# Two-layer hybrid decoder step on one core: gate and up units of the feed-forward as four token blocks of 264, sent in two pairs of seven block products

## The reference, cut to what matters

```python
h = _rmsnorm(x, P['norm_ffn_g'][layer]) * (1 + mod[:, 4]) + mod[:, 3]
gu = h @ P['ffn_w_gate_up'][layer]
x = x + mod[:, 5] * ((jax.nn.silu(gu[..., :FFN_HIDDEN]) * gu[..., FFN_HIDDEN:]) @ P['ffn_w_down'][layer])
```

## Time and profile before

| | |
|---|---|
| runs (3) | 2440.2 us median, 2438.15 to 2442.3 |
| span of the profiled execution, first to last instruction | 2437.2 us |
| PE busy | 2379.8 us, 98% |
| DVE, ACT, POOL busy | 1170.9, 694.2, 773.4 us |
| one turn of the loop in layer 1, from one up unit's end to the next's (1869.42 to 1934.81) | 65.4 us |

### The profile page before, as it was taken

The page is one execution under the profiler, slowest core; times in us unless marked ns, Lnnn a source line. Parts: engine busy times, 40 slices in busy tenths (PEclk is TensorE's granted clock), DMA queues, the critical chain, the costliest instruction groups (busy, mean ns, idle before and its releaser), DMA issues.

```text
span 2437.2 us, 37047 instructions
## 1 busy us (share of the span) xinstructions
PE 2379.8 (98%) x15703; PEld 2268.7 (93%) x15703; DVE 1170.9 (48%) x2223; ACT 694.2 (28%) x1056; POOL 773.4 (32%) x652
## 2 busy tenths in 40 slices
PE   7999999999999999999999999999999999999998
PEld 5998878578999999999999999999999999999998
DVE  5277653557434444434446321546544444444445
ACT  5112324426222222212224211144421222122224
POOL 3231111113334433333333332133343343333431
PEclk9999999989999999999999999999999999999999
DMA  9424443960222222222222688311111111111111
GB/s 313 157 68 145 126 132 103 312 210 23 70 87 87 68 72 70 87 70 87 87 70 70 216 283 302 104 37 35 35 53 52 36 52 52 37 51 52 53 53 72
DMA packets 163970, 249.12 MB, mean 102 GB/s; under 512 B 6165, under 2 KB 150826, under 8 KB 162527
## 3 DMA queue, kind: packets, MB, share of 16 engines
q1 hardware_dynamic: 150762, 179.29, 22.4%
q0 software_dynamic: 4784, 63.31, 7.5%
q10 hardware_dynamic: 8260, 4.15, 0.6%
HBM read 228.04 MB, written 62.54 MB: 119 GB/s over the span
## 4 chain that ended last, share of the span: by engine, by line
PE 78%; DVE 1%; ACT 1%; issue 0%; ACTq 0%; DVEq 0%
PE ps L2844 32%; PE ps L2884 12%; PE ps L2882 12%; PE ps L2883 11%; PE ps L3034 4%; PE ps L2988 3%; PE ps L3169 1%; PE ps L3057 1%; PE ps L3361 0%; PE ps L3204 0%; DVE x L1875 0%; PE ps L3378 0%; PE ps L3078 0%; PE ps L3071 0%; DVE tmp L2435 0%
## 5 line engine op out<-in xcount | busy, mean ns | idle before, releaser
L2844 PE MATMUL ps<-h_hi,w_slot 128*128 128x352 f32 x2112 | 537.6, 328 | 3.0 <-DVE acc_s L1966 1.4
L2635 POOL TENSOR_TENSOR w_slot<-w_raw,w_slot 128x512 fp32r<-128x512 f32 x240 | 304.1, 1300 | 679.5 <-DVE w_sum L2028 552.5
L2844 PE MATMUL ps<-f_hi,w_slot 128*128 128x352 f32 x1920 | 467.7, 323 | 0.0
L2884 PE MATMUL ps<-h_hi,w_slot 128*128 128x352 f32 x1280 | 413.0, 323 | 0.0
L2882 PE MATMUL ps<-h_hi,w_slot 128*128 128x352 f32 x1280 | 412.8, 323 | 0.0
L2883 PE MATMUL ps<-h_lo,w_slot 128*128 128x352 f32 x1280 | 411.2, 321 | 0.0
L1965 DVE SCALAR_TENSOR_TENSOR x<-ps,mod,x 128x704 f32<-128x704 f32 (+1 forms) x384 | 270.6, 747 | 288.0 <-PE ps L2844 287.6
L2844 PEld LDWEIGHTS ps<-h_hi,w_slot 128*128 128x128 f32 x2112 | 370.2, 188 | 22.0 <-issue 18.8
L2844 PE MATMUL ps<-h_lo,w_slot 128*128 128x352 f32 x1056 | 339.2, 321 | 0.0
L2844 PEld LDWEIGHTS ps<-f_hi,w_slot 128*128 128x128 f32 x1920 | 333.8, 188 | 4.9 <-issue 4.1
L2621 POOL TENSOR_TENSOR w_slot<-w_raw,w_slot 128x512 fp32r<-128x512 f32 x132 | 178.4, 1377 | 490.1 <-ACT w_slot L1389 481.7
(11 more groups left out here) (399 smaller groups left out, 3209.3 us busy)
## 6 DMA issues: line engine op xcount, KB each, us to landing
w_raw<-in_ada_w SPq DMA_DIRECT2D x48, 1024.0 KB, 5.6
w_raw<-in_ffn_w_gate_up SPq DMA_DIRECT2D x44, 1024.0 KB, 5.1
out_kv_sample<-in_cache_b_kv POOLq DMA_DIRECT2D x8, 4088.0 KB, 21.5
w_raw<-in_ffn_w_down SPq DMA_DIRECT2D x22, 1024.0 KB, 4.9
w_raw<-in_e_w_in SPq DMA_DIRECT2D x11, 1024.0 KB, 5.6
w_raw<-in_o_w_in SPq DMA_DIRECT2D x10, 1024.0 KB, 17.5
cache<-in_cache_b_kv SPq DMA_DIRECT2D x16, 512.0 KB, 6.4
out_kv_sample<-in_cache_b_kv POOLq DMA_DIRECT2D x8, 1016.0 KB, 9.9
```

The lines of the kernel that those rows point to most:

```text
L2635: pool.tensor_tensor(w_slot[slot_of(it.raw)][:, c], w_raw[it.raw.slot][:, c], w_slot[it.hi[0]].bitcast(F32)[:, c], ALU.subtract).then_inc( ...
L2844: mm = pe.matmul(big(t)[:, b, 0:BLK], wt, xt[:, k, b * BLK:b * BLK + BLK], start=(k == 0 and n == 0), stop=(k == K - 1 and n == 2))
L2884: return pe.matmul(bank(it, j), w_low, x_high, start=False, stop=last, skip_group_check=True)
```

## The change

`BLK` blocks in the gate and up units of groups 1 to 10 become four blocks of `QB` = 264 tokens. They form two pairs: pair 1 (blocks 2 and 3) and pair 0 (blocks 0 and 1). Each pair is done by seven products. A unit is then 14 products of 12 matmuls of 264, in the order P1, P4, P2, P5, P6, P7, P3 of pair 1, then the same of pair 0. A slot of weights is given back after P2 of pair 0, a slot of sums after P3 of pair 0. ACT and DVE handle the results pair by pair. The sums of tokens cover 528 tokens each. The second half of the plain up unit's result leaves later (`hidden_rest`, after `t_rest` and the gate's `w_split`). For room in SBUF, several buffers move, and the scratch for POOL's DMA descriptors is made 2048 bytes a partition. A new wait makes DVE's `token_sums` of layer 0 wait for stores issued long before, and POOL's load of the short-conv state wait for the last up unit. The diff, cut to its core (a line of three dots is a cut):

```diff
-PRODUCTS = 9
+PRODUCT_STEPS = tuple((number, pair) for pair in (1, 0) for number in (1, 4, 2, 5, 6, 7, 3))
+PRODUCTS = len(PRODUCT_STEPS)
+STEP_OF = {key: i + 1 for i, key in enumerate(PRODUCT_STEPS)}
+PAIRS = (1, 0)
+HIDDEN = ((1, 1), (1, 0), (0, 1), (0, 0))
+COMBINED = 12
 U2_MADE, U3_MADE, U4_MADE, C21_MADE, C22_MADE, C12_MADE = range(1, 7)
-D_DONE, D_LAST, P1_DONE, P4_DONE, P2_DONE, P5_DONE, P6_DONE, P7_DONE, P3_DONE = range(1, 10)
+RAWS_MADE, T_MADE, T_HI_DONE = 4, 10, 6
+T3_LOW, T4_LOW = 7, 9
...
         items.append(Item("t_low", layer=layer))
         dense("project", "ffn_w_gate_up", GROUPS, role="f_up", layer=layer, j=0)
+        first_up = items[-1]
         items.append(Item("t_rest", layer=layer))
         for g in range(1, GROUPS):
             down = Item("f_down", weights="ffn_w_down", col=g - 1, layer=layer, gate=5, j=g - 1, big=take("big", 8))
             up = seven("f_up", layer, g)
             sums_split(gate)
+            if g == 1:
+                items.append(Item("hidden_rest", of=first_up))
...
+        def weights_used(it):
+            return product_done(it, 2, 0)
...
-                release(slot_of(gate.raw), product_done(gate, P2_DONE))
-                release(gate.hi[0], product_done(gate, P2_DONE))
+                release(slot_of(gate.raw), weights_used(gate))
+                release(gate.hi[0], weights_used(gate))
...
+        B0, B1 = [[slice((2 * r + h) * QB, (2 * r + h + 1) * QB) for r in range(2)] for h in range(2)]
+        PAIR = [slice(2 * r * QB, 2 * r * QB + 2 * QB) for r in range(2)]
+        HALF = [slice(r * QB, r * QB + QB) for r in range(2)]
...
+            def copy_p1(it, to, r):
+                product(it, 1, r)
+                act.activation(to[:, 0, B1[r]], bank(it, 0), ACT.Copy).then_inc(p1_copied, 1)
+            def gate_straight(it, r):
+                product(it, 2, r)
+                act.activation(tmp[:, 0, B0[r]], bank(it, 0), ACT.Silu).then_inc(straight_left, 1)
+            def gate_combined(it, r):
+                act.wait_ge(*combined_at(it, r, C22_MADE))
+                act.activation(tmp[:, 1, PAIR[r]], tmp[:, 1, PAIR[r]], ACT.Silu)
+                act.wait_ge(*combined_at(it, r, C12_MADE))
+                act.activation(tmp[:, 0, B1[r]], tmp[:, 0, B1[r]], ACT.Silu).then_inc(gate_made, 1)
...
+                    copy_p1(it, tmp, 1)
+                    gate_straight(it, 1)
+                    copy_p1(it, tmp, 0)
+                    gate_combined(it, 1)
+                    gate_straight(it, 0)
...
+            def up_hidden(it, i):
+                r, m = HIDDEN[i]
+                act.wait_ge(hidden_made, 4 * (it.n // 2) + i + 1)
+                act.activation(f_hi[:, m, PAIR[r]], tmp[:, m, PAIR[r]], ACT.Copy).then_inc(hid_hi, 1)
+                    copy_p1(it, f_sum, 1)
+                    up_hidden(it, 0)
+                    copy_p1(it, f_sum, 0)
+                    up_hidden(it, 1)
+                    up_hidden(it, 2)
+                    up_hidden(it, 3)
...
+                    for r in PAIRS:
+                        act.activation(h_hi[:, 0:4, B1[r]], t3_raw[:, :, HALF[r]], ACT.Copy).then_inc(t_hi_done, 1)
+                    for i, r in enumerate(PAIRS):
+                        act.wait_ge(t_made, T_MADE * it.layer + T3_LOW + i)
+                        act.activation(t4_hi[:, :, HALF[r]], t4_raw[:, :, HALF[r]], ACT.Copy).then_inc(t_hi_done, 1)
...
+                product(it, 6, r)
+                dve.tensor_tensor(u, bank(it, p6), u, ALU.add).then_inc(combined_left, 1)
+                product(it, 7, r)
+                dve.wait_ge(*combined_at(it, r, U2_MADE))
+                dve.tensor_tensor(w, bank(it, p7), u, ALU.add).then_inc(combined_left, 1)
+                dve.tensor_tensor(u, bank(it, p5), u, ALU.add).then_inc(combined_left, 1)
+                dve.wait_ge(*combined_at(it, r, U3_MADE))
+                dve.tensor_tensor(v, bank(it, p4), w, ALU.add).then_inc(combined_left, 1)
+                dve.tensor_tensor(w, bank(it, p5), w, ALU.add).then_inc(combined_left, 1)
+                if up:
+                    dve.wait_ge(*combined_at(it, r, C22_MADE))
+                    dve.tensor_tensor(tmp[:, 1, PAIR[r]], to[:, 1, PAIR[r]], tmp[:, 1, PAIR[r]], ALU.mult).then_inc(hidden_made, 1)
+                product(it, 3, r)
+                dve.wait_ge(*combined_at(it, r, U4_MADE))
+                dve.tensor_tensor(u, bank(it, p3), u, ALU.add).then_inc(combined_left, 1)
+                if up:
+                    dve.wait_ge(*combined_at(it, r, C12_MADE))
+                    dve.tensor_tensor(tmp[:, 0, B1[r]], u, tmp[:, 0, B1[r]], ALU.mult).then_inc(hidden_made, 1)
+                    for i in (0, 1) if r else (2, 3):
+                        hidden_low(it, i)
...
+                        up_straight(it.of, 1)
+                        combined(it.of, to, 1)
+                        up_straight(it.of, 0)
+                    else:
+                        combined(it.of, to, 1)
...
+                    for i, r in enumerate(PAIRS):
+                        dve.wait_ge(t_hi_done, T_HI_DONE * it.layer + 3 + i)
+                        low(h_lo[:, 0:4, B1[r]], h_hi[:, 0:4, B1[r]], t3_raw[:, :, HALF[r]]).then_inc(t_made, 1)
+                    for i, r in enumerate(PAIRS):
+                        dve.wait_ge(t_hi_done, T_HI_DONE * it.layer + 5 + i)
+                        low(t4_low[:, :, HALF[r]], t4_hi[:, :, HALF[r]], t4_raw[:, :, HALF[r]]).then_inc(t_made, 1)
...
+                    of_weights(0, 0, 0, tokens(0, B0[1]), split_waits=True)
+                    left_before(it, C21_MADE)
+                    pe.wait_ge(t_made, T_MADE * it.layer + T4_LOW)
+                    for q in (2, 3):
+                        pe.wait_ge(part_made, 4 * it.r + q + 1)
+                    of_weights(1, 4, 1, of_sum(t4_hi, t4_low, 1))
+                    pe.wait_ge(p1_copied, 2 * it.n + 1)
+                    of_weights(0, 4, 0, tokens(4, B0[1]), adds=True)
+                    of_sums(2, 0, of_sum(t_hi[:, 0], t1_low, 1))
                     big_evacuated(pe, before)
+                    left_before(it, C22_MADE)
+                    of_sums(3, 1, of_sum(t_hi[:, 1], t2_low, 1))
+                    of_sums(4, 2, tokens(0, B1[1]))
+                    left_before(it, C12_MADE)
+                    of_sums(5, 3, tokens(4, B1[1]))
+                    pe.wait_ge(straight_left, 2 * it.n + 1)
+                    of_weights(0, 0, 0, tokens(0, B0[0]))
+                    pe.wait_ge(*combined_at(it, 1, C21_MADE))
+                    pe.wait_ge(t_made, T_MADE * it.layer + T4_LOW + 1)
+                    of_weights(1, 4, 1, of_sum(t4_hi, t4_low, 0))
+                    pe.wait_ge(p1_copied, 2 * it.n + 2)
+                    of_weights(0, 4, 0, tokens(4, B0[0]), adds=True)
                 else:
+                    of_sums(3, 0, of_sum(t_hi[:, 0], t1_low, 0))
+                    of_sums(4, 1, of_sum(t_hi[:, 1], t2_low, 0))
+                    pe.wait_ge(*combined_at(it, 1, C22_MADE))
+                    of_sums(2, 2, tokens(0, B1[0]))
+                    pe.wait_ge(*combined_at(it, 1, C12_MADE))
+                    of_sums(5, 3, tokens(4, B1[0]))
...
-    nc = bacc.Bacc("TRN2", target_bir_lowering=False, num_devices=1)
+    nc = bacc.Bacc("TRN2", target_bir_lowering=False, num_devices=1, dynamic_dma_scratch_size=2048)
```

More of the change, by code:

```diff
@@ L1085, in build_trunk @@
                         raw_of[u0 + 2] = claim_raw()
[L1086 to L1087 removed]
+                release(up.sums[0], sums_used(up))
+                release(up.sums_hi[0], sums_used(up))
                 if g + 1 < GROUPS:
@@ L1588, in up_products @@
                 if half == 0:
-                    if last:
-                        act.wait_ge(straight_left, 3 * it.n + 2)
-                        act.activation(f_hi[:, :, B2], tmp[:, 0:2, B2], ACT.Copy).then_inc(hid_hi, 1)
-                    product(it, P1_DONE)
-                    act.activation(f_sum[:, 0, B1], bank(it, 2), ACT.Copy).then_inc(p1_copied, 1)
-                else:
-                    c = slice(0, 2 * BLK if last else TOK)
-                    for i, m in enumerate((1, 0)):
-                        act.wait_ge(hidden_made, it.n + i)
-                        act.activation(f_hi[:, m, c], tmp[:, m, c], ACT.Copy).then_inc(hid_hi, 1)
+                    copy_p1(it, f_sum, 1)
@@ L1714, in _ @@
                         split_hi(it.unit + 1)
-                    for m in range(2):
+                    for m in range(1 if it.role == "f_up" else 2):
                         leave(it, m)
@@ L1967, in evacuate_tile @@
                     .then_inc(big_free[t % 2], 1)
-            def product(it, which):
-                dve.wait_ge(*product_done(it, which))
-            def up_straight(it):
-                dve.wait_ge(gate_made, it.n // 2 + 1)
-                for m in range(2):
-                    product(it, D_DONE + m)
```

(35 more changed lines are left out.)

232 lines of the change are left out of this document (94 added, 138 removed).

## The result

The changed kernel takes 2527.2 us (median of 4 runs, 2524.26 to 2530.15), beside 2441.3 for the kernel before in the same session (4 runs, 2438.15 to 2443.91): 1.0351 of its time, interval 1.0336 to 1.0365. It is slower, as forecast, by 86 us where 56 were forecast.

The account below looks back on a forecast made before the run. PE's issue alone was taken to set the loop's time. Per layer, 13.4 us saved against waits of 41.3 and 0.2 gave +28.1, twice +56: 2496 us, chance 0.66, own range 2475 to 2520, wider range 2448 to 2545.

Parts of the forecast that it names:

- The distance: Gate and up units: matmuls of 264 columns 122 ns apart, a unit 20.50 us in place of 21.17.
- The floor rival: Gate and up units: matmuls at 112.5 ns, other engines' chains then set the loop; 2448 us, chance 0.07.
- the shared loads: Gate and up units: weight loads count with the tokens, 131 ns a matmul; 2541 us, chance 0.10.
- the fixed distance: Gate and up units: 160 ns a matmul whatever its length, units of 26.9 us; about 2690 us, chance 0.05.
- Wait 1: Each gate unit's end: PE waits for the down weights' low pieces, 1.74 us, 10 times a layer, 17.4 us.
- Wait 2: Gate unit's start behind an up unit: P2 waits for ACT's copy of P1, 1.92 us, 9 times a layer.
- Wait 3: Start of each layer's loop: P2 starts at 9.55 us in place of 2.93, costing 6.6 us a layer.
- the clock: PE's clock dropping after the waits at the two layer starts: taken as 0, upper end 14 us.
- The last down product: Wait ahead of each layer's last down product, put at 0.2 us a layer.
- What costs nothing: DVE's and ACT's shorter operations, wider token sums, new waits, moved buffers and smaller scratch: 0 us, scratch 0 to 10.
- The sum: Whole kernel: per layer 13.4 us saved, waits 41.3 and 0.2, net +28.1, twice +56; 2496 us, 2.3% slower.
- The rival of covered waits: Loop: parts ready sooner, the gate units' start and end waits vanish, layer-start wait stays; 2427 us, chance 0.12.

Follow-up runs that it names:

- The run with zeros: Changed kernel with POOL writing zeros in place of the four low pieces of the gate weights, gate units 2 to 10: 2499.5 us, 1.0232 of before.
- the run with shorter pieces: Changed kernel with POOL making the gate weights' low part, groups 2 to 10, in eight pieces of 256 elements, not four of 512: 2561.7 us, 1.0491 of before.
- the best kernel: The kernel with the raw weights first, plus another start of each layer's loop (fourth sum's parts first, then the third): 2413.9 us, 0.9874 of before.
- the kernel with the raw weights first: Changed kernel with P1, P4, P2 of both pairs ahead of the sums' products in each unit, banks dealt anew: 2419.5 us, 0.9901 of before.

## Why the prediction was right, and where its size was off

**The distance: right.** 121.5 ns measured, 122 taken. The 122 was a choice between 120 and 123.3 that no row decided, so that it came out within 0.5 ns is in part luck. From 352 to 264 columns the distance falls from 160.1 to 121.5, 0.44 ns a column. The floor rival (112.5), the shared loads (131) and the fixed distance (160) are refuted by the up unit alone. The rule of the Trainium skill ("TensorE: Matmul & The Clock Gate", Back-to-back issue gap) that was weighed ahead of the result gave 112.5 ns; the trace disagrees, by 9 ns at 264 as by 11 at 352. That section calls it the gap of isolated matmuls and says that in a stream with weight loads both set the spacing, which the prediction left out. At 121.5 ns a unit takes 20.41 us and saves 0.75; the forecast was 0.67.

**Wait 1: right.** Forecast 1.74 us at twenty first down tiles, measured 1.70, and 31.7 us came back when it was taken away.

**Wait 2: the mechanism right, its size off, and this is the step that failed.** I forecast 1.92 us for a gate unit and 3.05 were measured; times 18 this is 20 of the 30 us that I was short. The term is "0.93 for it (1.33 at 704, three quarters and the overlap)" and the last product behind it. They measured 1.60 and 1.04. The row of 1.33 us in the earlier trace rows could not be scaled by its columns. It starts at 1934.93, and POOL's last piece ends at 1930.49 + 5.03 = 1935.52, 0.74 us before the product ends. The same product with POOL idle stands in the profile before, behind the last up unit of layer 1 (timeline of DVE):

```profile
2391.67 0.89 DVE L2001 TENSOR_TENSOR tmp<-f_sum,tmp 128x704 f32<-128x704 f32 x1
```

So the row held 0.44 us of waiting for POOL, of which I took three quarters, and I gave the last product, undisturbed in that row's stage, no waiting at all. In the changed kernel both products fall on POOL's pieces. The run with zeros shows this by taking POOL away (0.71 and 0.43, P2 1.5 us earlier), the run with shorter pieces by shortening what DVE waits for. P4's own wait, which I had put at 1.0 us and inside the other, came to 1.63 for the same reason from POOL's side; it stayed inside the chain to P2 and did not delay it.

**Wait 3: nearly right.** Forecast 6.6 us a layer. The first gate unit of layer 0 was 6.9 us longer than an up unit, that of layer 1 8.1. PE's rows in layer 0:

```profile
630.60 0.48 PE L2939 MATMUL ps<-t_hi,w_slot 128*128 128x264 f32 x1 [3.46 <-DVE t_low L2122]
630.88 0.42 PE L2940 MATMUL ps<-t_low,w_slot 128*128 128x264 f32 x1
...
635.18 0.39 PE L2939 MATMUL ps<-h_hi,w_slot 128*128 128x264 f32 x1 [1.68 <-ACT tmp L1609]
635.40 0.28 PE L2940 MATMUL ps<-h_lo,w_slot 128*128 128x264 f32 x1
```

Behind 3.46 us of idle time PE ran at 220 ns a matmul for one product. I had taken nothing for the clock, of 0 to 14 us. In layer 0 it did cost nothing, since the next wait, for ACT, absorbed it. In layer 1 a second product ran slowly behind the second wait, 1.2 us. P2 starts 9.67 us behind the unit's start in both layers, where 9.55 were forecast.

**The last down product: missed.** I gave it 0.2 us a layer, and it waits 1.5 (L3102 in the list of waits). It is wait 1 again, for the same chain behind P2 of pair 0 of the last up unit. I had the chain and didn't apply it there.

**What costs nothing: right.** The scratch was run alone. In the best kernel DVE's and ACT's added operations are covered throughout the loop.

**The sum.** Measured, for the 85.1 us of the span: 40 x 0.75 = 30 saved, and 34.0 (20 x 1.70), 54.9 (18 x 3.05), 15.0 (6.9 + 8.1) and 3.0 lost, so +76.9. The other 8.2 us lie, by the starts of the stages in both traces, in five places. 1.2 are ahead of the first loop, a stage whose end differs by more than that from profile to profile. 3.4 are in the gate and up units: behind the two waits of a gate unit the second matmul comes 0.08 and 0.11 us later than the normal distance, and I had not counted that. 1.9 are in the stages between the units (1.7 of them in layer 0), 0.7 between the two loops and 1.0 behind the last one; of these three the cause is open. The rival of covered waits named the right bar (both waits of a turn together below 1.35 us): the turn saves 1.5 and waited 4.75. With another order they are covered, and the kernel is then 1% faster than before.

## What to carry to other kernels

When a change shortens the bounding engine's part, list each chain of the other engines with its slack, at every place where the same chain occurs, the last one too; where buffers are handed on in a ring, put the work that frees the contended buffer first. A duration read while another engine ran beside may hold a wait: look at where it ends against the other engine's instructions before scaling it. And splitting the matmul finer pays only down to the distance that shorter matmuls no longer undercut: 111 ns here, for 88 to 176 columns. That the weight loads set this distance fits it, and no run here changed the loads.

## What the runs showed of the hardware

- A DVE operation with both inputs in SBUF was held while POOL's running operation, which also reads SBUF, went on, and POOL's next one was longer in its turn. At the border shown, POOL's third piece runs from 1924.43 to about 1925.7. DVE's product starts at 1924.68 and ends at 1926.28, some 0.6 us after this piece, and the fourth piece takes 1.75 us in place of 1.29. Operations that read one input from PSUM kept their 0.42 us beside the same pieces, and beside POOL's writing of zeros the product kept its 0.71. The Trainium skill ("SBUF — State Buffer", Who interferes with whom) says that a DVE instruction with two SBUF inputs contends with a GpSimd instruction that reads SBUF, not with one that only writes it, and calls the port pair that the two share an exclusive lock. The trace agrees, save that some 0.14 us of the product's 0.71 passed beside the third piece. The shortened pieces (0.71 and 0.52 in place of 1.60 and 1.04, the first with DVE ahead of POOL's piece) speak against an even sharing.
- The distance of matmuls with full weights, each with its own load: 160.1 ns at 352 columns, 121.5 at 264, 111.3 at 176, 132 and 88 mixed.
- TensorE's clock did not follow from the length of one idle time. After 3.46 and 3.51 us, at the two layers' starts of the changed kernel, PE issued 264 columns every 220 ns at a granted clock of 0.50, the second time only from 0.6 us after it had gone on. After 3.2 us, with the shorter pieces, it did so in 14 of 18 gate units and in four not at all. After 2.03 us, in the kernel with the raw weights first, it did so in layer 0, from 0.8 us after it had gone on and for some 15 matmuls, and in layer 1 not. After 1.2 to 1.7 us the clock never fell, more than fifty times in the changed kernel, not even where two of these stood 1.5 us apart.
